# Last layer: the results of three head groups are turned back by VectorE's 32x32 squares and two transfers, and read five units later

## The reference, cut to what matters

```python
def fox_layer(x, norm_w, w_in, q_norm_w, out_norm_w, w_out, k, v, F):
    h = rmsnorm(x, norm_w)
    proj = h @ w_in                                    # 2048 -> 4096
    q = proj[..., :D_MODEL].reshape(B, T, FOX_HEADS, FOX_HDIM)
    gate = proj[..., D_MODEL:]
    q = head_rmsnorm(q, q_norm_w).transpose(0, 2, 1, 3)
    o = forgetting_attention(q, k, v, F)
    o = head_rmsnorm(o.transpose(0, 2, 1, 3), out_norm_w.reshape(FOX_HEADS, FOX_HDIM))
    o = o.reshape(B, T, D_MODEL) * jax.nn.silu(gate.astype(jnp.float32))
    return x + (o.astype(x.dtype) @ w_out)
```

## Time and profile before

| what | value |
|---|---|
| median of three runs | 1828.47 us (1828.24 to 1828.49) |
| the profiled execution's own time | 1828.43 us |
| its span from the first to the last instruction | 1826.6 us |
| TensorE busy | 1813.7 us, 99% |
| VectorE busy | 1267.3 us, 69% |
| ScalarE busy | 942.7 us, 52% |
| granted TensorE clock | full speed in every slice |
| the four runs of `l3_q` on TensorE | 1522.8 to 1729.3 us, the last three 53.4 us each |

### The profile page before, as it was taken

How to read it: one execution, slowest core, us unless ns; L and a number is a source line. 1 busy time by engine, 2 the same in 40 slices (tenths; PEclk the granted TensorE clock), 3 DMA queues, 4 the chain that set the end, 5 groups by cost and what they waited for, 6 DMA issues and landing times.

```text
span 1826.6 us, 24598 instructions
## 1 busy us (share of the span) xinstructions
PE 1813.7 (99%) x8999; PEld 1531.1 (84%) x8999; DVE 1267.3 (69%) x1711; ACT 942.7 (52%) x1310; POOL 38.0 (2%) x116
## 2 busy tenths in 40 slices
PE   8999999999999999999999999999999999999999
PEld 7899998888888888887888888888888888888887
DVE  6676766588556755767887878787767556577764
ACT  4545554455465555636554545555435444565542
POOL 2000000000000004000000000000000000000000
PEclk9999999999999999999999999999999999999999
DMA  8565454668889887575555555544547776555453
GB/s 293 162 177 148 139 175 156 202 179 185 177 153 212 175 179 176 191 238 159 174 175 152 167 173 154 179 154 160 185 138 232 217 217 209 162 160 163 159 166 113
DMA packets 172909, 323.61 MB, mean 177 GB/s; under 512 B 16584, under 2 KB 23136, under 8 KB 172048
## 3 DMA queue, kind: packets, MB, share of 16 engines
q1 hardware_dynamic: 171680, 317.89, 60.6%
q10 hardware_dynamic: 576, 4.19, 0.6%
q0 software_dynamic: 560, 0.26, 0.1%
HBM read 318.11 MB, written 4.19 MB: 176 GB/s over the span
## 4 chain that ended last, share of the span: by engine, by line
PE 98%; DVE 1%; ACT 0%; DMA 0%; issue 0%; DVEq 0%
PE acc L366 28%; PE acc L368 28%; PE acc L367 27%; PE ps L615 2%; PE ps L2760 2%; PE ps L463 1%; PE acc L332 1%; PE acc L333 1%; PE acc L331 1%; PE ps L648 1%; PE acc L350 0%; PE acc L349 0%; PE acc L353 0%; PE acc L355 0%; PE acc L348 0%; PE acc L354 0%
## 5 line engine op out<-in xcount | busy, mean ns | idle before, releaser
L299 DVE TENSOR_TENSOR wlo<-wraw,whi 128x1024 fp32r<-128x1024 f32 x579 | 699.1, 1222 | 337.4 <-ACT whi L284 334.4
L284 ACT ACTIVATE whi<-wraw 128x1024 fp32r<-128x1024 f32 x579 | 599.9, 1052 | 365.8 <-PE acc L368 333.4
L366 PE MATMUL acc<-whi,ta_hi 128*128 128x512 f32 x1664 | 659.7, 396 | 3.6 <-DVE ta_lo L548 2.0
L368 PE MATMUL acc<-whi,ta_lo 128*128 128x512 f32 x1664 | 649.2, 390 | 0.0
L367 PE MATMUL acc<-wlo,ta_hi 128*128 128x512 f32 x1664 | 647.8, 389 | 0.0
L366 PEld LDWEIGHTS acc<-whi,ta_hi 128*128 128x128 f32 x1664 | 312.6, 188 | 68.7 <-DVE ta_lo L548 3.4
L368 PEld LDWEIGHTS acc<-whi,ta_lo 128*128 128x128 f32 x1664 | 312.3, 188 | 66.9
L367 PEld LDWEIGHTS acc<-wlo,ta_hi 128*128 128x128 f32 x1664 | 312.8, 188 | 62.1
L366 PE MATMUL acc<-whi,tb_hi 128*128 128x512 f32 x576 | 228.4, 396 | 0.0
L368 PE MATMUL acc<-whi,tb_lo 128*128 128x512 f32 x576 | 224.9, 390 | 0.0
L367 PE MATMUL acc<-wlo,tb_hi 128*128 128x512 f32 x576 | 224.4, 390 | 0.0
(11 more groups left out here) (325 smaller groups left out, 1644.8 us busy)
## 6 DMA issues: line engine op xcount, KB each, us to landing
wraw<-in_ml_w_in SPq DMA_DIRECT2D x129, 512.0 KB, 5.8
wraw<-in_a_w_in SPq DMA_DIRECT2D x128, 512.0 KB, 3.9
wraw<-in_kv_w SPq DMA_DIRECT2D x64, 512.0 KB, 4.0
wraw<-in_b_w_in SPq DMA_DIRECT2D x64, 512.0 KB, 4.4
wraw<-in_mla_w_in SPq DMA_DIRECT2D x49, 512.0 KB, 4.6
wraw<-in_mla_w_out SPq DMA_DIRECT2D x32, 512.0 KB, 3.8
wraw<-in_ml_w_out SPq DMA_DIRECT2D x32, 512.0 KB, 4.4
wraw<-in_a_w_out SPq DMA_DIRECT2D x32, 512.0 KB, 3.8
```

Source lines behind the costliest of these rows:

```text
L284: nc.scalar.activation(unit_of(whi, n, SPLIT, w), unit_of(wraw, n, RAW, w), ACT.Copy).then_inc(w_high, 1)
L299: nc.vector.tensor_tensor(unit_of(wlo, n, SPLIT, w), unit_of(wraw, n, RAW, w), unit_of(whi, n, SPLIT, w).bitcast(F32), ALU.subtract).then_ ...
L366: nc.tensor.matmul(o, xh, wh, start=first, stop=False)
L368: m = nc.tensor.matmul(o, xl, wh, start=False, stop=end)
```

## The change

For groups 0 to 2 (`by_squares`) the 8 transposes of TensorE are gone. VectorE transposes the 32x32 squares of `o3` right behind the gate, at u = 25, into the space of the scores (`o3_stage`, over `S3` and part of `PT3`). SP writes that to memory (`back_squares`) at unit 2 of its load order in the run after next and reads it back into `o3` in the turned order at unit 4. VectorE's and ScalarE's part of `back` moves from u = 28 to u = 33, which is unit 1 of the run after next; VectorE reads `o3` instead of PSUM. TensorE no longer waits for `lo` before it turns the queries. Group 3 is turned by TensorE as before. VectorE's `mask_max` of the next group waits until the staged tile has been written out, and `l3_out` waits for groups 0 and 1 at its unit 0 and for group 2 at its unit 4. The second run is written out, so that the loop covers two runs.

```diff
+        def by_squares(g):
+            return not (isinstance(g, int) and g == 3)
+        def back_at(g):
+            return L3_AT["back"] + (5 if by_squares(g) else 0)
+        BACK_OUT, BACK_IN = 2, 4
...
+            def turn_back(g, p):
+                if p == BACK_OUT:
+                    sp.wait_ge(l3["b_sq"], TB * (g + 1))
+                    sp.dma_start(back_squares, o3_stage).then_inc(l3["b_out"], 16)
+                if p == BACK_IN:
+                    sp.wait_ge(l3["b_out"], 16 * (g + 1))
+                    for j in range(4):
+                        sp.dma_start(o3_flat[32 * j:32 * j + 32, :].rearrange("q (i r) -> q i r", i=4),
+                                     back_squares.rearrange("(i q) (j r) -> j q i r", i=4, j=4)[j]).then_inc(l3["b_in"], 16)
...
# ScalarE, and VectorE alike
-                if u == L3_AT["back"] + LAG:
+                if u == back_at(g) + LAG:
                     back()
...
                 step(act, high, evac, "l3_q", p, it, ("l3_q", it - 1))
+                    q_side(it - 2, p + 2 * length("l3_q"))
                     q_side(it - 1, p + length("l3_q"))
                     q_side(it, p)
...
# VectorE, at the end of post
                     nc.vector.tensor_tensor(flat(o3), flat(gw3), flat(o3), ALU.mult).then_inc(l3["og"], 1)
+                    if by_squares(g):
+                        dve.wait_ge(l3["og"], g + 1)
+                        blocks = o3_stage.rearrange("p (j b h c) -> p b j h c", j=4, b=TB, h=4)
+                        for b in range(TB):
+                            nc.vector.transpose(blocks[:, b], square_columns(o3[:, b, :])).then_inc(l3["b_sq"], 1)
# VectorE, in back
+                        if by_squares(g):
+                            dve.wait_ge(l3["b_in"], 64 * (g + 1))
+                            y = o3_flat.rearrange("p (i b h c) -> p b h i c", i=4, b=TB, h=4)
+                            w = colB[:, group(64, g)].unsqueeze(2).unsqueeze(3).to_broadcast([P, 4, 4, 32])
+                            nc.vector.tensor_tensor(t.rearrange("p k (i c) -> p k i c", i=4), y[:, b], w,
+                                                    ALU.mult).then_inc(l3["tmp"], 1)
+                            continue
# VectorE, before mask_max of sc0
+                    if not first(g):
+                        dve.wait_ge(l3["b_out"], 16 * g)
...
# TensorE
-                    if g > 0:
-                        pe.wait_ge(l3["lo"], 2 * g)
...
-                if u == L3_AT["back"]:
+                if u == L3_AT["back"] and not by_squares(g):
                     back()
...
                 if p == 0:
+                    pe.wait_ge(l3["lo"], 4)
+                if p == 4:
                     pe.wait_ge(l3["lo"], 6)
```

More of the change, by code:

```diff
@@ L72, in then, with enter, leave @@
         self.sync()
-    def enter(self, it, per):
+    def enter(self, it, per, at=1):
         self.it, self.per, self.start = it, per, self.n
-        self.n -= per
-    def leave(self, runs):
-        assert self.n + self.per - self.start == self.per, (self.n + self.per - self.start, self.per)
+        self.n -= at * per
+    def leave(self, runs, at=1):
+        assert self.n + at * self.per - self.start == self.per, (self.n + at * self.per - self.start, self.per)
         self.n = self.start + runs * self.per
@@ L937, in build @@
         l3 = sems(3, "r_dg r_row f_row f_e f_ok sq_out kss qss oss ksq kv_ krs kn kt kT qsq qv qrs qn qt qT sc msk mx ex pt ptc pv o "
-                     "ge gs sq v rs on og ogp tmp hi lo")
+                     "ge gs sq v rs on og ogp b_sq b_out b_in tmp hi lo")
         def dst_l3(name, k, b, it):
@@ L988, in build @@
                  "v3": 22, "post": 22, "back": 25}
+        def by_squares(g):
[3 more added lines that the diff above has]
+        BACK_OUT, BACK_IN = 2, 4
+        back_squares = nc.dram_tensor("back_squares", (P, 2 * COLS), F32).ap()
+        o3_flat = o3.rearrange("p b n -> p (b n)")
+        o3_stage = bass.AP(S3.tensor, S3.offset, [list(S3.ap[0]), [1, 2 * COLS]])
         def fox_qk(c, b):
@@ L1043, in _ @@
                             turn_keys(3, p)
-                    with sp.Fori(1, runs) as it:
+                    for p in range(units(tiles)):
+                        load(name, p, 1)
+                        if name == "l3_kv":
+                            turn_keys(0, p)
+                    with sp.Fori(2, runs) as it:
                         for p in range(units(tiles)):
@@ L1048, in _ @@
                                 turn_keys(it - 1, p)
+                            else:
+                                turn_back(it - 2, p)
                 elif runs == 1:
@@ L1051, in _ @@
                         load(name, p)
+                        if name == "l3_out":
+                            turn_back(2, p)
                 else:
@@ L1639, in _ @@
                 q_side(0, p)
-            with act.Fori(1, 4) as it:
+            for p in range(length("l3_q")):
+                step(act, high, evac, "l3_q", p, 1, ("l3_q", 0))
+                q_side(0, p + length("l3_q"))
+                q_side(1, p)
+            with act.Fori(2, 4) as it:
                 for p in range(length("l3_q")):
                     step(act, high, evac, "l3_q", p, it, ("l3_q", it - 1))
+                    q_side(it - 2, p + 2 * length("l3_q"))
                     q_side(it - 1, p + length("l3_q"))
@@ L1646, in _ @@
                 step(act, high, evac, "l3_out", p, 0, ("l3_q", 3))
+                q_side(2, p + 2 * length("l3_q"))
                 q_side(3, p + length("l3_q"))
@@ L2443, in back @@
                         t = tmpT[:, b, :].rearrange("p (k t) -> p k t", t=P)
-                        dve.wait_ge(l3["ogp"], 2 * g + b + 1)
+                        if by_squares(g):
[5 more added lines that the diff above has]
+                            continue
+                        dve.wait_ge(l3["ogp"], b + 1)
                         nc.vector.tensor_tensor(t, ps[:, b, :].rearrange("p (k t) -> p k t", t=P),
@@ L2484, in _ @@
                 q_side(0, p)
-            with dve.Fori(1, 4) as it:
-                own.enter(it, L3_OWN)
+            for p in range(length("l3_q")):
+                step(dve, low, evac, "l3_q", p, 1, ("l3_q", 0))
+                q_side(0, p + length("l3_q"))
+                q_side(1, p)
+            with dve.Fori(2, 4) as it:
+                own.enter(it, L3_OWN, 2)
                 for p in range(length("l3_q")):
                     step(dve, low, evac, "l3_q", p, it, ("l3_q", it - 1))
+                    q_side(it - 2, p + 2 * length("l3_q"))
                     q_side(it - 1, p + length("l3_q"))
                     q_side(it, p)
-            own.leave(3)
+            own.leave(2, 2)
             for p in range(length("l3_out")):
                 step(dve, low, evac, "l3_out", p, 0, ("l3_q", 3))
+                q_side(2, p + 2 * length("l3_q"))
                 q_side(3, p + length("l3_q"))
```

## The result

| | before | after |
|---|---|---|
| median | 1828.48 us | 1831.66 us |
| range of the undisturbed runs | 1828.21 to 1828.60 | 1831.49 to 1831.90 |
| ratio | 1 | 1.0018, 95% interval 1.0011 to 1.0024 |
| span of the profiled execution | 1826.6 us | 1830.1 us |

One of the 20 runs of each kernel was disturbed (9918.57 us before; 1875.21 us after, at a granted clock of 0.923) and is left out of the ranges. The changed kernel is slower by 3.2 us (2.0 to 4.4 by the interval's ends). The forecast was 1832.8.

A forecast was written before the change was run, and what follows sets the result against it. TensorE, busy 99% of the span, was taken to bound the kernel. To the median of 1828.47 us came 3.1 us for VectorE's queue, removed turn included, and 1.2 for ScalarE's copy: 1832.8 us, range 1828.5 to 1836.0.

The forecast's parts named there:

- The larger chance, 0.60: Chance given to the changed kernel being slower by over 0.2%, which begins at 1832.1 us.
- The gain: TensorE's removed transposes: 0.88 us a group, 2.6 us for three, if nothing else changes.
- The first cost: VectorE's two transposes ahead of unit 10 delay `low` up to unit 12: +1.03 us a group, gain included, +3.1 in all.
- The second cost: `back` at unit 1 delays ScalarE's copy for `v0`: 0.40 us a group, +1.2 us in all.
- The transfers at nothing: Writing the squares to memory and reading them back, 10.6 us out and back, was costed at nothing.
- The cover of 7 us: Time between squares in `o3`, by about 1668, and VectorE wanting them, after 1675.0; lateness beyond it costs TensorE equally.
- VectorE's wait alone: Rival: ScalarE's copy stays hidden and only VectorE's delay of +3.1 us counts, 1831.6 us; chance 0.17.
- Everything hidden: Rival: `low` of units 10 and 12 end no later than TensorE comes, 1825.9 us, not slower; chance 0.10.
- squares late: Rival: transfers stretch past about 18 us and VectorE waits at unit 1, 1838.8 us at 2 us beyond; chance 0.05.
- the larger first term: Rival: transposes or a slower multiplication nearer their upper bounds, 1834.7 to 1836 us; chance 0.13.

The follow-up runs named there:

- e9: Changed kernel with the transposes behind the `low` of unit 12, `back` behind ScalarE's copy, and the next group's `norm` one unit later: 1825.24 us.
- e5: Kernel before with VectorE's two transposes added behind the gate for groups 0 to 2, result unused, TensorE's turn kept: 1832.38 us.
- e6: Changed kernel without VectorE's two transposes, transfers kept and waiting for the gate: 1827.79 us.
- e10: Changed kernel with only the next group's `norm` one unit later: 1829.37 us.
- e2: Changed kernel with `back` one unit later, on ScalarE behind the copy that `v0` waits for: 1830.88 us.
- e8: Kernel before without VectorE's and ScalarE's part of `back` for groups 0 to 2, TensorE's turn kept: 1827.78 us.
- e4: Changed kernel without the write to memory, the read back and the waits for them: 1831.43 us.
- e1: Changed kernel with VectorE's transposes moved from behind the gate to behind the `low` of unit 12, transfers two units later: 1829.90 us.
- e7: Changed kernel with the squares' read back issued at unit 9 of SyncE's load order instead of 4: 1858.61 us.

## Why the prediction was right, and where it was off

The direction, the range and both costs held: 1831.66 us against 1832.8, in a range from 1828.5 to 1836.0. The sum was 4.3 us and 3.2 were measured. One step failed, and it is told below. The signs came as well: TensorE's idle time at units 10 and 12 (1.00 and 0.61 us by the starts, 1.1 and 0.6 forecast), the wait ahead of `v0`, and no wait of VectorE for its transfer. A run takes 54.4 us from `v0` to `v0` where it took 53.35; 54.8 was forecast.

The larger chance, 0.60, stood on slower by over 0.2%. The measured 0.18% lies just inside, where 0.38 stood. It is clear of no change all the same (0.11 to 0.24%), so the 0.2% that the prediction took as what can be told was too wide.

**The gain.** 0.88 us for a turn. e9, in which TensorE shows no wait, gives 3.1 us: 3 x 0.88 and 0.5 of what is told next.

**The first cost, 1.03 a group: 0.98 measured.** The delay of `low` at unit 12 was worked out as 1.32 and is 1.32 (13.46 us behind `v3` before, 14.78 after). Only TensorE's start behind a late `low` was too large: it took 0.14 from layer 0, and here it is 0.06 and 0.05 (1656.49 + 1.18 against 1657.73; 1662.65 + 1.22, the usual length of a `low`, against 1663.92). Why these places differ no run shows. e5 and e6 confirm the cost from both sides, e10 shows that the chain runs through `norm` as the prediction followed it.

**The second cost, 0.40 a group: 0.29 measured**, 0.26 by e2. Each step of the chain on ScalarE came within 0.02 of its row: the rounding 0.82 behind the multiplication, then 1.13, 0.95 and 0.57. The end that I averaged away was right: of 0.30 (the load hidden) and 0.49 the lower, with 0.05 instead of 0.14 at the restart and 0.1 for the slow first steps.

**The step that failed**: "Three turns of VectorE and ScalarE at unit 12 leave that place too. They did not hold TensorE there, so nothing is gained by it", and with it "I found no wait of TensorE anywhere". They did not hold it at unit 12, but at unit 13: the `low` that stands behind `back` started at 1664.33, ended at 1665.55, and TensorE's unit 13 started at 1665.61, where 0.79 behind the queries' turn, 1665.43, would have been its time. The matmuls' view shows no wait there, since the modelled ends hide it; the weight loads' view does. Leaving gives 0.2 us a group back, shown by e8 and by the account.

So of the 1.1 us by which the sum was too large, the overlooked gain is 0.7, the second cost 0.3 and the first 0.1.

**The transfers at nothing**: right (e4). The cover of 7 us, some 6 as measured, was not wide, though: two units later, as in e1, the squares are late.

**The rivals.** The nearest in number was VectorE's wait alone, 1831.6, but for the wrong reason: ScalarE's copy is late, by e2, and the gain at unit 13 hides it in the sum. Everything hidden, squares late and the larger first term did not occur. e9 shows that the first of these was open to a kernel with three steps in other places, not to this one.

## What to carry to other kernels

When an engine that bounds the time is relieved of work by one that is 69% busy, look up the stretch that receives the work: here VectorE had 0.4 us to spare at unit 12, and 1.3 us put there cost more than the 0.88 they saved, while the same 1.3 us behind the `low` of unit 12, with a `norm` out of the way, cost nothing (e9). Moving work away also frees what stood behind it; look for the gain at the next consumer, in the weight loads' waits and the distances between starts, not in the matmuls' idle time alone. A reordered queue is checked on each engine it passes, since ScalarE's copy, and not the multiplication that was moved, was what TensorE came to wait for.

## What the runs showed of the hardware that was not expected

A stop of TensorE of 6.7 us (e7) takes the granted clock from 1.00 to 0.50, that is from 2.4 to 1.2 GHz, and the half clock stays for some 6 us of work behind it, until 1639. Behind the second stop it stays for 3 us, behind the third for 5; why these differ no run shows. The three stops cost 6.6 us beside the 20.7 waited. The stops of 1.0 and 0.6 us in the changed kernel left it at 1.00, in the stretch of the first:

```profile
1656.00:1658.00 2.00, 1.17 (x5) 0.67 (x5) 2.00 (x3) 0.00 (x0) 0.00 (x0) 1.00 0.00 0
```

The Trainium skill, TensorE: Matmul & The Clock Gate, section "What's actually happening", says that a gate ahead of the array lets through fewer clock pulses after inactivity and all of them again after work; with that e7 agrees.
